# A hybrid attention layer on one Trainium2 core: every product of 512 columns reads its moving columns from two halves in turn

## The reference

```
h = RMSNorm(x);  proj = h @ w_in
A: sliding-window attention (8 heads of 64, window 128), with sinks
B: index scores  sum_h w[t,h] relu(q_idx[t,h].k_idx[s]);  the best 256 keys of each token;
   attention of 8 heads over those keys, one shared key and value of 64 from a latent of 128
merged = sigmoid(gate_a) * (o_a @ w_branch_a) + sigmoid(gate_b) * (o_b @ w_branch_b)
x = x + merged @ w_out
x = x + (silu(n @ w_ffn_gate) * (n @ w_ffn_up)) @ w_ffn_down     with n = RMSNorm(x), 2816 wide
out = RMSNorm(x)
```

## Time and profile before

| | |
|---|---|
| median of 3 runs (lowest to highest) | 3171.73 us (3170.11 to 3173.22) |
| the profiled execution: time, span | 3170.38 us, 3168.6 us |
| mean granted TensorE clock | 0.999 |
| PE busy (instructions) | 3129.9 us, 99% of the span (15706) |
| PEld busy | 2664.1 us, 84% |
| DVE, ACT, POOL busy | 1820.2, 1419.6, 2028.9 us |
| DMA | 392.61 MB, mean 124 GB/s |

### The profile page before, as it was taken

One profiled execution on the slowest core, in us unless ns is written; L12 is line 12 of the kernel. 1 busy time (PEld: TensorE's weight loads), 2 busy tenths in 40 slices (PEclk: granted clock), 3 DMA queues, 4 the chain that ended last, 5 costly groups with the idle time before them and its releaser, 6 DMA issues.

```text
span 3168.6 us, 44080 instructions
## 1 busy us (share of the span) xinstructions
PE 3129.9 (99%) x15706; PEld 2664.1 (84%) x15706; DVE 1820.2 (57%) x3706; ACT 1419.6 (45%) x2589; POOL 2028.9 (64%) x2201
## 2 busy tenths in 40 slices
PE   9999999999999999999999999999999999999999
PEld 8888888888878888888888888988888799888887
DVE  3336656547655546557666756977868589421111
ACT  3324445435454434245454534836655378320101
POOL 5766766655566666755666675376667822766666
PEclk9999999999999999999999999999999999999999
DMA  5766464455534333323533333163333500532333
GB/s 154 205 169 176 123 181 132 133 144 169 180 103 142 108 109 100 117 99 107 175 109 110 99 116 117 42 236 96 104 106 113 175 16 16 186 93 94 100 100 100
DMA packets 464202, 392.61 MB, mean 124 GB/s; under 512 B 29264, under 2 KB 394064, under 8 KB 463344
## 3 DMA queue, kind: packets, MB, share of 16 engines
q1 hardware_dynamic: 442544, 345.56, 36.1%
q10 hardware_dynamic: 21440, 44.22, 3.8%
HBM read 323.76 MB, written 62.81 MB: 122 GB/s over the span
## 4 chain that ended last, share of the span: by engine, by line
PE 92%; DVE 2%; POOL 2%; ACT 2%; issue 1%; DMA 1%; SPq 0%; ACTq 0%; DVEq 0%; POOLq 0%
PE BANK L1054 21%; PE BANK L1056 21%; PE BANK L1055 21%; PE LP L1054 4%; PE LP L1056 4%; PE LP L1055 4%; PE BANK L1335 3%; PE BANK L1360 2%; PE LP L1315 2%; PE LP L1316 2%; PE LP L1171 2%; PE LP L1170 2%; PE BANK L1362 2%; POOL WLO L991 1%; POOL WHI L989 1%
## 5 line engine op out<-in xcount | busy, mean ns | idle before, releaser
L991 POOL TENSOR_TENSOR WLO<-WRAW,WHI 128x512 fp32r<-128x512 f32 x912 | 1224.6, 1343 | 76.2
L989 POOL TENSOR_SCALAR WHI<-WRAW 128x512 fp32r<-128x512 f32 x912 | 622.2, 682 | 752.7 <-PE BANK L1056 594.9
L1054 PE MATMUL BANK<-H2hi,WHI 128*128 128x512 f32 x1376 | 538.7, 392 | 1.0 <-POOL WLO L991 0.9
L1055 PE MATMUL BANK<-H2lo,WHI 128*128 128x512 f32 x1376 | 535.9, 389 | 0.0
L1056 PE MATMUL BANK<-H2hi,WLO 128*128 128x512 f32 x1376 | 535.8, 389 | 0.0
L1054 PE MATMUL BANK<-HThi,WHI 128*128 128x512 f32 (+1 forms) x1024 | 393.4, 384 | 1.2 <-DVE QS L2076 0.9
L1056 PE MATMUL BANK<-HThi,WLO 128*128 128x512 f32 (+1 forms) x1024 | 388.3, 379 | 0.0
L1055 PE MATMUL BANK<-HTlo,WHI 128*128 128x512 f32 (+1 forms) x1024 | 388.2, 379 | 0.0
L1783 ACT ACTIVATE MASK<-SCD,THR 128x896 bf16<-128x896 f32 (+5 forms) x186 | 281.9, 1516 | 191.2 <-DVE THR L2136 163.1
L1056 PEld LDWEIGHTS BANK<-H2hi,WLO 128*128 128x128 f32 x1376 | 258.3, 188 | 54.4
L1054 PEld LDWEIGHTS BANK<-H2hi,WHI 128*128 128x128 f32 x1376 | 258.5, 188 | 53.1 <-issue 1.3
(11 more groups left out here) (330 smaller groups left out, 6477.4 us busy)
## 6 DMA issues: line engine op xcount, KB each, us to landing
WRAW<-in_w_in SPq DMA_DIRECT2D x124, 512.0 KB, 4.4
WRAW<-in_w_ffn_gate SPq DMA_DIRECT2D x88, 512.0 KB, 3.8
WRAW<-in_w_ffn_up SPq DMA_DIRECT2D x88, 512.0 KB, 3.8
WRAW<-in_w_ffn_down SPq DMA_DIRECT2D x88, 512.0 KB, 3.5
qsp<-QS SPq DMA_DIRECT2D x32, 512.0 KB, 5.8
WRAW<-in_w_out SPq DMA_DIRECT2D x32, 512.0 KB, 4.6
gates<-GS ACTq DMA_DIRECT2D x62, 256.0 KB, 2.3
GL<-gates ACTq DMA_DIRECT2D x48, 256.0 KB, 4.2
```

Source lines behind the costliest of these rows:

```text
L989: nc.gpsimd.tensor_scalar(hi, raw, 1.0, 1.0, ALU.mult, ALU.mult).then_inc(w_hi, 1)
L991: nc.gpsimd.tensor_tensor(lo, raw, hi.bitcast(f32), ALU.subtract).then_inc(w_split, 1)
L1054: nc.tensor.matmul(dst, whi, mhi, start=first, stop=False)
L1055: nc.tensor.matmul(dst, whi, mlo, start=False, stop=False)
```

## The change

It brings four things.

- The moving operand of every product with keys, attention results, the second norm and the weights of the output and down products is read `by_turns`. Of a part of a 512-column stretch of keys, `keys_by_turns` takes the first columns of both halves.
- Where a bank must come out in the old order, the stored order changes: the copies and subtractions that write `OThi`, `OTlo`, `KIhi`, `KIlo`, `KBShi` and `KBSlo` read their source with a step of two elements (`parted`) and write two contiguous halves (`sides`). For `H2hi` and `H2lo` each instruction for 256 columns becomes one that writes two runs of 128.
- The bank of a row product comes out with its columns interleaved, and `add_row` reads it `parted`. The hidden activations `FFhi` and `FFlo` have their tokens interleaved, and the down product loads its 128 weight columns with a step of two elements (`row_tile`).
- `forms` is gone.

```diff
+        def sides(t):
+            return t.rearrange("p (s c) -> p s c", s=2)
+        def parted(t):
+            return t.rearrange("p (c s) -> p s c", s=2)
+        def keys_by_turns(t, a, v):
+            return by_turns(t[:, a:a + ROWS])[:, 0:v // 2, :]
...
-                    hi, lo = (by_turns(t[:, s, :]) if t in (HThi, HTlo) else t[:, s, :] for t in (mhi, mlo))
+                    hi, lo = (by_turns(t[:, s, :]) for t in (mhi, mlo))
...
-                        last = three(dst[:, :], hi[:, e, c * P:(c + 1) * P], lo[:, e, c * P:(c + 1) * P], OThi[s][:, e, :],
-                                     OTlo[s][:, e, :], e == 0, e == ET - 1)
+                        last = three(dst[:, :], hi[:, e, c * P:(c + 1) * P], lo[:, e, c * P:(c + 1) * P], by_turns(OThi[s][:, e, :]),
+                                     by_turns(OTlo[s][:, e, :]), e == 0, e == ET - 1)
...
+                def row_tile(t, s, j):
+                    return (t[:, s, j * P:(j + 1) * P] if stage == ("wo",)
+                            else parted(t[:, s, :])[:, j % 2, j // 2 * P:(j // 2 + 1) * P])
...
-                            last = three(dst[j][:, :], shi[:, s, r], slo[:, s, r], hi[:, kk, :], lo[:, kk, :],
-                                         s == 0, s == len(part) - 1)
+                            last = three(dst[j][:, :], row_tile(shi, s, j), row_tile(slo, s, j), by_turns(hi[:, kk, :]),
+                                         by_turns(lo[:, kk, :]), s == 0, s == len(part) - 1)
...
-                        nc.tensor.matmul(dst[:, a - c:a - c + v], q, KIhi[:, a:a + v], start=True, stop=False)
+                        nc.tensor.matmul(dst[:, a - c:a - c + v], q, keys_by_turns(KIhi, a, v), start=True, stop=False)
...
-                        hi, lo = H2hi[:, s, r], H2lo[:, s, r]
+                        hi, lo = (by_turns(h[:, s, :])[:, t * P:(t + 1) * P, :] for h in (H2hi, H2lo))
...
-                nc.scalar.copy(OThi[s][:, e, :], (OTA, OTB)[s][:, e, :]).then_inc(oh_ready, made(oh_ready, (b, s, e)))
+                nc.scalar.copy(sides(OThi[s][:, e, :]), parted((OTA, OTB)[s][:, e, :])).then_inc(oh_ready, made(oh_ready, (b, s, e)))
...
-                            last = nc.scalar.activation(H2hi[:, k, r], bk[:, 2 * i * P:2 * (i + 1) * P], ACT.Copy, scale=G2[:, k:k + 1])
+                            last = nc.scalar.activation(sides(H2hi[:, k, :])[:, :, r], sides(bk[:, 2 * i * P:2 * (i + 1) * P]), ACT.Copy,
+                                                        scale=G2[:, k:k + 1])
...
-                    c = X1[:, j, half * ROWS:(half + 1) * ROWS]
-                    nc.vector.tensor_tensor(c, rows_bank(stage, b, half, j)[:, :], c, ALU.add
+                    c = sides(X1[:, j, half * ROWS:(half + 1) * ROWS])
+                    nc.vector.tensor_tensor(c, parted(rows_bank(stage, b, half, j)[:, :]), c, ALU.add
```

More of the change, by code:

```diff
@@ L1126, in rows @@
                                      (count, 3), (count + 1, 2), (count + 1, 3)]:
-                            w, r = (i + q - count) % 2, slice(j * P, (j + 1) * P)
+                            w = (i + q - count) % 2
                             hi, lo = (t[w][:, :, :].rearrange("p (k s) c -> p k (s c)", k=2) for t in (WHI, WLO))
@@ L1132, in rows @@
                                     pe.wait_ge(w_split, 2 * (i + q - count) + kk + 1)
-                                last = three(dst[j][:, :], shi[:, s, r], slo[:, s, r], hi[:, kk, :], lo[:, kk, :],
-                                             False, s == len(part) - 1)
+                                last = three(dst[j][:, :], row_tile(shi, s, j), row_tile(slo, s, j), by_turns(hi[:, kk, :]),
+                                             by_turns(lo[:, kk, :]), False, s == len(part) - 1)
                             if q > count or j == JT - 1:
@@ L1835, in project @@
                 for s in range(2):
-                    nc.scalar.copy(KIhi[s * HD:(s + 1) * HD, rows], bk[0:HD, :]).then_inc(k_hi, made(k_hi, (b, "ki", s)))
+                    nc.scalar.copy(sides(KIhi[s * HD:(s + 1) * HD, rows]), parted(bk[0:HD, :])).then_inc(k_hi, made(k_hi, (b, "ki", s)))
                 act.wait_ge(k_ready, n(k_ready, (b, "ki", 1)))
@@ L2526, in lower_half @@
                 def lower_half(t, p):
[L2527 removed]
+                    r = slice(t * P, (t + 1) * P)
                     dve.wait_ge(h_hi, n(h_hi, (b, 1, t, p)))
```

52 lines of the change are left out of this document (14 added, 38 removed).

## The result

The changed kernel takes 3096.63 us (median of 4 runs, 3093.58 to 3099.18); the kernel before, run beside it, 3170.94 us (4 runs, 3170.11 to 3173.22). The ratio is 0.9763, interval 0.9752 to 0.9775. A second set of runs gave 3094.79 us and 0.9748 (0.9735 to 0.9761). The forecast was 3079 us, in 3070 to 3092. So the change is faster by 74 to 77 us where 92 were forecast, and both medians lie above the range; less than 80 us was also the prediction's own sign of being wrong. The profiled execution took 3094.78 us (span 3093.0, granted clock 0.997).

A forecast was written before the change was run, and what follows sets the result against it. PE was taken to bound the kernel, by number of products times pitch. Products 84.2, keys 7.3, narrower products 4, minus 3 for new waits, made 92.5 us less: 3079 us, range 3070 to 3092.

The forecast's parts named there:

- the prediction's own sign of being wrong: Whole kernel: the prediction is wrong if the time falls by less than 80 us.
- 84 us by pitch: Second norm, down, branch and output products: 7776 products of 512 columns, each 10.8 ns shorter, 84 us less.
- 9.3 were set for their keys: Index scores and mixer B logits: 7.3 us less for 512-column key products, plus 2 us for narrower keys.
- the end: End of kernel: removing `forms`, 28 products in some 6 us beside final additions and result writing, counted as 0.
- Rival 1: Down products: by-turns order with stepped weights costs 48.3 ns each above stored order, giving 3204 us; chance 3%.
- Rival 2: All converted products: a new SBUF line for every column slows 8672 products, 419 us more, some 3590 us; chance 1%.
- I take 0, as the cover is there: Step-two reads and writes on ACT, DVE and POOL: priced at 0, since they fit beside PE's work.
- Rival 4: Stepped reads double ACT, DVE and POOL times; 14 us at additions and first attention-result splits, giving 3093 us; chance 5%.
- 3 us of new waits: Dense stretches where POOL is busiest: PE's added waits for suppliers such as `WLO`, 3 us more.
- rival 3: Densest stretches of the first three blocks: POOL or DVE takes over, 11.5 us lost, giving 3090 us; chance 9%.
- POOL's 4.05 us against a job's 5.18: Per job of 24 products: POOL needs 4.05 us, PE 5.18 us after the change, so POOL is late nowhere.
- a granted mean of 0.999: PE's clock over the span: granted mean 0.999, the full 2.4 GHz, so it doesn't part the two pitches.

The follow-up runs named there:

- The run with short passes: Changed kernel with the counting passes of the search for best keys cut to half the scores' width in block 2, a quarter in block 3: 3084.57 us, 0.9731.

## Why the prediction was too low

*Right.* PE's pitch was the quantity that gave the gain. The three products of a job have 215.8 ns in all stages (84 us by pitch); projections with scores and attention brought 10.1 us where 9.3 were set for their keys; the end brought nothing, and the run without `forms` shows it. That 9.3 and 10.1 lie so near is in part luck: key products of 512 columns had a pitch of 231 to 233 ns before (the earlier trace rows have `KIhi` at 396 ns, where the down products have 390), so by their mean pitch the keys gained some 15 us, and some 5 us were lost beside them. The additions stayed at 0.69 us, and the other reads of banks at step two cost nothing (`KIhi` and `KBShi` on ACT 578 and 588 ns, unchanged). Rival 1 is wrong for this kernel, since both orders together have the short pitch; but its suspicion has a core, for stepped weights do cost 6 ns beside the stored order. Rival 2 didn't happen: no converted form has a longer pitch than before. The Trainium skill's rule behind it (SBUF — State Buffer, Specifications) thus doesn't describe these reads.

*Wrong: "I take 0, as the cover is there"*, for reads at step two on ACT, DVE and POOL. For banks it held. For the split of the attention results, which reads SBUF while PE already reads by turns, it measured 6.7 us: 1.7 per branch stage. Rival 4 had 2 us for this place in each block, but as twice the work of every such read, which no median showed. The cause is the change's own: the new order of PE's reads makes the new step of the others' reads expensive. I priced each edit by itself and never the two side by side. The stored reads run beside PE without loss, and the cover was thinner than I took it: PE consumes the results as they are split.

*Wrong in size: "3 us of new waits".* Block 2 alone misses 5.7 us in gate and up, 2.1 in its output product and 2.2 between its stages; the ends of the down products 1.9, block 3's output 0.9. This is rival 3, with 11.5 us set for it at 9%, and it came true, with 10.0 us, in one block of three and on top of the rest. I had counted POOL's 4.05 us against a job's 5.18 and looked at POOL's busiest stretch. The run with short passes, 10 to 12 us faster, shows that the search was what was tight in block 2, by the waits on DVE, and that its slack in the kernel before had been just enough, since there the same edit brought nothing. The cause of what is left at the ends of the down products and in block 3's output product stays open.

*Not priced: the clock.* I took a granted mean of 0.999 as given. The changed kernel has 0.996 to 0.998, by the estimate above about 2 us.

Together: 6.7 for the split, 3.1 for the output products, 5.7 and 1.9 for block 2 and the down products' ends, 1.1 for the other gate and up stages and 2.3 between stages, less 0.8 that projections and attention brought beyond the keys' term and less the 3 that I had set: 17 us, which is 92.5 less 75.6. In the profiled execution the two added falls of the clock lie in the projections and in the attention of block 0, inside the row that still gained 10.1. The range was too narrow above: 3092 held one of the two losses, and both came.

## What to carry to other kernels

Where PE is the bound at 99%, a shorter pitch may not be gained in full, as here: count, stage by stage, what every supplier has to spare, since the slack was spent in the densest block. A new order of access is to be priced together with what reads the same memory at that time, and put where it is free: here in the reads of banks and in the weight columns, not in a copy from SBUF. Where one product's two operands both change their step, measure the pair; each alone may cost what both together don't.

## What the runs showed of the hardware

- A float32 product of 512 moving columns has a pitch of 215.8 ns when these come from two halves in turn, with contiguous or stepped weight columns; 226.7 ns as stored, but 231 to 233 in most products with keys (the cause is not shown); 233 ns as stored with weight columns at step two.
- A read of 128x512 elements of SBUF at step two, alone: ACT 642 ns, DVE 682. Beside PE's read by turns at full clock: ACT 852 to 888 ns, four in 3.21 us; DVE up to 837, four in 3.06. Beside PE's read as stored at full clock: ACT four in 2.37 us (with DVE beside), DVE four in 2.50. Beside PE's read by turns at a clock of 0.50, DVE's four took 2.49 us.
- POOL's first split of 128x512 elements took 2.59 us instead of 0.61 beside a scan on DVE, in the kernel before and in the changed one.
